# A decoder layer on one core: 35 weight-remainder subtractions move from VectorE to GpSimd

## The reference

```python
def decoder_layer(x, c, ...):
    mod = (jax.nn.silu(c) @ w_ada + b_ada)[:, None, :]
    sh1, sc1, g1, sh2, sc2, g2 = jnp.split(mod, N_MOD, axis=-1)
    h = x * (1 + sc1) + sh1
    proj = h @ w_in
    q, k, v, u, gates = jnp.split(proj, [...], axis=-1)    # 1024, 1024, 1024, 512, 2048 columns
    q = rope(q.reshape(bt, s, N_HEADS, 2, HEAD_DIM), pos)  # 8 heads, 2 x 64 dims
    k = rope(k.reshape(bt, s, N_HEADS, 2, HEAD_DIM), pos)
    o = attend(q, k, v, lam)        # softmax(q1 k1) - lam * softmax(q2 k2), causal, times v
    attn_out = (head_rmsnorm(o, subln_g) * (1.0 - lam_init)).reshape(bt, s, ATTN_WIDTH)
    pool_out, new_pool = pool_mixer(pool_buf, u, start_pos, w_pool, pool_scale)
    g_pool, g_attn = jnp.split(jax.nn.sigmoid(gates), N_BRANCHES, axis=-1)
    merged = g_pool * pool_out + g_attn * attn_out
    x = layer_norm(alpha * x + (1 + g1) * (merged @ w_out), ln1_g, ln1_b)
    h2 = x * (1 + sc2) + sh2
    x = layer_norm(alpha * x + (1 + g2) * hier_moe(h2, ...), ln2_g, ln2_b)   # 16 experts, top 2
    return x, k, v, new_pool
```

## Time and profile before

| | |
|---|---|
| median of 3 runs | 1476.77 us (1475.71 to 1477.59) |
| the profiled execution: its time, its span | 1477.59 us, 1475.8 us |
| PE matmuls busy | 1282.6 us, 87% |
| DVE busy | 1007.4 us, 68% |
| ACT busy | 732.2 us, 50% |
| POOL busy | 221.4 us, 15% |
| transfers | 229.41 MB |

### The profile page before, as it was taken

One profiled execution on the slowest core, in us unless ns is written; L12 is line 12 of the kernel. 1 busy time (PEld: TensorE's weight loads), 2 busy tenths in 40 slices (PEclk: granted clock), 3 DMA queues, 4 the chain that ended last, 5 costly groups with the idle time before them and its releaser, 6 DMA issues.

```text
span 1475.8 us, 24543 instructions
## 1 busy us (share of the span) xinstructions
PE 1282.6 (87%) x8756; PEld 1115.0 (76%) x8756; DVE 1007.4 (68%) x1508; ACT 732.2 (50%) x1285; POOL 221.4 (15%) x132
## 2 busy tenths in 40 slices
PE   6789979999999999999999978899199999999700
PEld 3478879999999989989989856678178887888500
DVE  1432537667585775758677574685759998999579
ACT  1334333555454544545455544222148998999512
POOL 1432110000000000000000024564211111111150
PEclk9999989999999999999999989999569999999955
DMA  9687332223332322333223443452077897557393
GB/s 310 184 279 252 112 98 85 85 83 93 100 109 64 103 84 81 102 101 89 75 82 91 129 128 103 119 210 115 28 285 276 321 355 288 190 196 252 140 283 135
DMA packets 210979, 229.41 MB, mean 155 GB/s; under 512 B 17942, under 2 KB 184794, under 8 KB 210747
## 3 DMA queue, kind: packets, MB, share of 16 engines
q1 hardware_dynamic: 195627, 173.39, 37.5%
q0 software_dynamic: 6976, 25.23, 5.2%
q10 hardware_dynamic: 8280, 29.51, 5.0%
HBM read 173.07 MB, written 46.79 MB: 149 GB/s over the span
## 4 chain that ended last, share of the span: by engine, by line
PE 74%; DVE 11%; ACT 4%; DMA 4%; issue 3%; SPq 2%; POOL 1%; ACTq 0%; DVEq 0%; POOLq 0%
PE AB L983 10%; PE AB L987 10%; PE AB L984 10%; PE S L910 6%; PE S L912 6%; PE S L911 6%; PE S L1079 4%; ACT F L1447 3%; PE T L1105 2%; PE OB L910 2%; ACT R L1447 1%; PE OB L911 1%; PE OB L912 1%; PE S L925 1%; DMA F<-y_d,slot 1%
## 5 line engine op out<-in xcount | busy, mean ns | idle before, releaser
L1447 ACT ACTIVATE R<-F 128x1024 fp32r<-128x1024 f32 (+4 forms) x305 | 292.7, 1006 | 95.9 <-DVE F L2003 46.7
L983 PE MATMUL AB<-R 128*128 128x344 f32 x960 | 315.9, 333 | 0.0
L984 PE MATMUL AB<-R 128*128 128x344 f32 x960 | 304.7, 321 | 0.0
L910 PE MATMUL S<-R 128*128 128x512 f32 x480 | 193.6, 403 | 1.8 <-ACT F L1447 1.6
L912 PE MATMUL S<-R 128*128 128x512 f32 x480 | 189.2, 394 | 0.0
L911 PE MATMUL S<-R 128*128 128x512 f32 x480 | 189.0, 394 | 0.0
L983 PEld LDWEIGHTS AB<-R 128*128 128x128 f32 x960 | 182.0, 190 | 3.4 <-issue 3.2
L984 PEld LDWEIGHTS AB<-R 128*128 128x128 f32 x960 | 182.3, 190 | 1.7 <-issue 1.7
L987 PE MATMUL AB<-R 128*128 128x344 f32 x960 | 171.6, 321 | 0.0
L1447 ACT ACTIVATE F<-AB 128x344 f32<-128x344 f32 (+1 forms) x126 | 56.0, 447 | 215.2 <-PE AB L987 214.6
L987 PEld LDWEIGHTS AB<-R 128*128 128x128 f32 x960 | 155.7, 188 | 0.0
(11 more groups left out here) (275 smaller groups left out, 2406.3 us busy)
## 6 DMA issues: line engine op xcount, KB each, us to landing
F<-in_w_ada SPq DMA_DIRECT2D x24, 1024.0 KB
F<-in_w_in SPq DMA_DIRECT2D x44, 512.0 KB, 4.0
F<-in_w_e_gate SPq DMA_DIRECT2D x16, 1024.0 KB, 6.0
F<-in_w_e_up SPq DMA_DIRECT2D x16, 1024.0 KB, 10.7
F<-in_w_e_down SPq DMA_DIRECT2D x16, 1024.0 KB
y_d<-F ACTq DMA_DIRECT2D x32, 512.0 KB
out<-F SPq DMA_DIRECT2D x24, 512.0 KB, 4.1
F<-F SPq DMA_DIRECT2D x192, 43.0 KB, 1.9
```

The lines of the kernel that those rows point to most:

```text
L910: mm(out, w[0], m[1], start=start, stop=False)
L983: mm(bank[:, 0:PIECE], whl[b][0][:, k, :], x[1][:, k, :], start=(k == 0), stop=False)
L984: mm(bank[:, 0:PIECE], whl[b][0][:, k, :], x[0][:, k, :], start=False, stop=False)
L1447: return nc.scalar.activation(out, in_, func, **kw)
```

## The change

The function `chunk_lo` and its calls are removed from DVE's list. POOL's loop over `chunk_rest`, which ended with chunk 4, now runs to chunk 39. The operation, its operands, its two waits before it and the semaphore after it stay what they were, but POOL comes to a chunk as soon as ACT has split it, and not after the maxima of the next block.

```diff
@@ DVE
-        def chunk_lo(h, i):
-
-            for g in step_pieces(h, i):
-                c = g // 3 + 2
-                if g % 3 == 2 and c < N_CHUNKS:
-                    if c == 5:
-                        dve.wait_ge(w_lo.sem, U_CHUNKS + 5)
-                    dve.wait_ge(w_landed[c % 2], raw_landed(c))
-                    dve.wait_ge(w_hi.sem, U_CHUNKS + c + 1)
-                    TT(whl[c % 2][1], wraw2[c % 2], whl[c % 2][0].bitcast(F32), ALU.subtract).then_inc(w_lo.sem, 1)
-
         for g in range(6):
             rope(g)
         operands_qk(0)
@@ DVE, in the loop over h and i
                 maxima(h, i)
-                if i:
-                    chunk_lo(h, i - 1)
-                elif h:
-                    chunk_lo(h - 1, 7)
                 if i == 0:
@@ POOL
-        for c in range(1, 5):
+        for c in range(1, N_CHUNKS):
             chunk_rest(c)
```

## The result

The changed kernel takes 1489.44 us (median of 5 runs, 1485.78 to 1492.56) against 1476.85 us before: a ratio of 1.0083, interval 1.0061 to 1.0104. It is slower by 12.6 us. The profiled execution took 1488.52 us with a span of 1486.3 us, 10.5 us more than the one of before.

What follows compares the result with a forecast made beforehand. PE was taken to bound the attention loop; its only gain, 7 x 0.15 = 1.0 us in block 7, gave 1476.77 - 1.0 = 1475.8 us, a forecast of no change. Its own range was 1474 to 1479, the wider one 1472 to 1480 us.

Steps and rivals of the forecast that it cites:

- The bound: Attention loop: PE is busy 86.82 of 87.90 us a head; a perfect DVE could give at most 8.1 us.
- what was removed: 35 subtractions, 42.5 us, leave DVE; only block 7 of each head helps PE, 7 x 0.15 = 1.0 us.
- The layout of the meetings: POOL's subtractions laid block by block into a head: DVE held 2.1 + 1.7 us, nothing lost on PE's path.
- rival 2: Block 2: line 2094 doesn't move forward and is held, 2.0 us late; up to +4.6, 1481.4 us; chance 0.05 (or another holding).
- Rival 3: Attention loop: DVE's relief also shortens PE's waits for ACT, at most all 8.1 us, 1468.7 us; chance 0.06.
- By the row at 928.98 DVE wins with a lead of 0.01 us: Block 6: line 2129, 0.03 us ahead of POOL, was expected to win as line 2295 did before the change.
- Rival 1: Block 6: POOL wins, line 2129 is held and PE waits 1.2 us a head; +7.4, 1484.2 us; chance 0.12.
- 70 us of holding: Estimate from the skill's port rule: up to 35 x 2.0 us put on DVE, more than the 42.5 us taken off.

## Why the prediction was wrong

**The bound, and what was removed: right.** PE is the bound of the loop and the relief of DVE is worth what it does to PE in block 7. That term was 0.15 us a head, and a head without the holding takes 87.74 us instead of 87.90: 0.16. The low parts of `w_in` were never late: no row of any profile shows PE waiting for them.

**The layout of the meetings: right in every block but for who wins.** Block 1: line 2119 was forecast to be held to no effect.

```profile
307.19 2.40 POOL L2526 TENSOR_TENSOR R<-F,R 128x1024 fp32r<-128x1024 f32 x1 [16.72 <-ACT R L1447]
307.47 2.13 DVE L2119 TENSOR_TENSOR sm<-sm 128x1 f32<-128x1 f32 x1
312.11 0.28 PE L910 MATMUL OB<-R 128*128 128x256 f32 x1
...
322.46 1.22 DVE L2094 TENSOR_TENSOR R<-F,R 128x1024 fp32r<-128x1024 f32 x1
323.52 2.41 POOL L2526 TENSOR_TENSOR R<-F,R 128x1024 fp32r<-128x1024 f32 x1 [13.93 <-ACT R L1447]
```

In these rows of DVE, POOL and PE after the change the short instruction takes 2.13 us, and PE's product has no wait. (In the first head it is the next instruction of the combine that is held there, line 2128, 0.35 us before:)

```profile
221.82 2.40 DVE L2128 TENSOR_SCALAR F<-F,sm 128x256 f32<-128x256 f32 x1
```

Block 2: line 2094 has moved forward and is ahead of POOL by 1.06 us, so rival 2 did not come about. Rival 3 neither: the waits for ACT are the same to the tenth.

**The step that failed** is "By the row at 928.98 DVE wins with a lead of 0.01 us", applied to line 2129 in block 6. The lead itself was worked out to the hundredth. But the row was that of an instruction with a constant as its scalar, and line 2129 reads its scalar from SBUF. With a constant in its place the same instruction wins at the same lead of 0.03 us; with its own scalar it needs more than 0.04 and no more than 0.06. So the record's start is not yet the moment at which DVE claims the shared ports, and that moment depends on the operands. (That DVE reads the scalar first, and claims the ports after it, is the natural reading of the two runs, and the 0.06 us by which the form with the scalar from SBUF is longer fits the lead that it needs; what happens inside is not seen.)

**Rival 1's price was right, its chance was not.** It was priced at 1.2 us of PE's wait a head, 1.05 with the gain taken off. Measured are 1.36 (89.10 against 87.74) and 1.20; its sum gave 7.4 us where the seven heads lost 8.4. It had 0.12, for a margin of 0.03 us read off by analogy; with seven meetings alike, a margin that thin deserved nearly even odds.

**Two meetings were missed.** In block 4 the lead of 0.16 us was taken to hold in every head; in the fourth, DVE is some 0.2 us later and it costs 1.1 us. (It waits there for PE's line 1105, as shown above; why in this head alone, while PE's rows stand at the same places as in the head before, no run shows.) And the last head, which the change doesn't touch, was left out: POOL's first subtraction for `w_out` slid onto line 2162 and held it for 2.0 us in three of the four profiles of the changed kernel. The prediction had read from its rows that nothing is held on instructions with one input, but those rows are of instructions that read PSUM; lines 2162 and 2128 have one tensor as input too, from SBUF, and are held. From the seventh head's block 6 to the end of attention the profile has 115.11 us instead of 112.31; less the 1.2 of that block 6 this is 1.6. The sum is 8.4 + 1.1 + 1.6 = 11.1 us, which is the growth of attention in the profile (706.70 to 717.76); from that to the 12.6 us of the medians is within the spread of the runs.

The Trainium skill's rule ("SBUF — State Buffer", section "Who interferes with whom"), that whoever issues first blocks the other for its whole instruction, holds in all these rows: 2.0 to 2.2 us of holding by a subtraction of 2.4 us, 0.3 by one of 0.46. But to tell who issues first the start of the records is good only to some 0.05 us. The estimate that the prediction made from it, 70 us of holding, was high, since 20 of the 35 subtractions hold nothing: DVE's busy time shows 35 us, and PE felt some 10 of them.

## What to carry to other kernels

Before work goes from VectorE to GpSimd, lay each moved instruction beside VectorE's instructions that read SBUF, those with one tensor as input included (lines 2128 and 2162 were held as the combine was), and ask of each meeting what waits behind the one that loses; a total of busy time tells nothing. Where the order hangs on less than 0.1 us, take it as undecided or fix it by a wait: here a wait in block 6, on a semaphore that was already there, turned 0.83% slower into no loss, and with waits in blocks 1 and 4 and in the last head as well, it became 0.16% faster. And look at the stages behind the change too, since they shift against each other.

## What the runs showed that was not expected

A VectorE instruction with a scalar read from SBUF was held with its record 0.03 us ahead of GpSimd's (3.38 us instead of 1.15), the same instruction with a constant won with the same 0.03 us (1.09 us, GpSimd 3.32 instead of 2.40), and with 0.06 us ahead the first form won too. And a holding need fall neither on a long instruction nor on one with two tensors as inputs: a one-column product of 0.16 us took 2.13, a scaling of one tensor of 16 partitions 2.33 instead of 0.34, one of 128x256 2.40 instead of 0.35.
